# Down projection of a decoder block in split fp32: every fourth weight residual formed by an accumulating DMA

## The chip, the cores and the metric

One core of one Trainium2 chip. The metric is the device time of one execution in microseconds (us), the median over runs. The engines are TensorE (PE), VectorE (DVE), ScalarE (ACT), GpSimd (POOL) and SyncE (SP), each with its own queue of instructions; 16 DMA engines move data between HBM and the on-chip memory.

## The reference, cut to what matters

A decoder block on x of 256 x 2048, float32: a token-mixing part with three branches, then an MLP with a squared ReLU.

```python
h = rmsnorm(x, norm_ffn_g[l])
x = x + jnp.square(jax.nn.relu(h @ w_up[l])) @ w_down[l]
return rmsnorm(x, final_g)
```

`w_up` is 2048 x 8192 and `w_down` 8192 x 2048. The change touches only the product with `w_down`.

## The kernel before

**Split weights.** Each float32 operand is split into a rounded part (type float32r) and the residual. A product is the sum of three: rounded times rounded, rounded times residual, and residual times rounded. Weights come from HBM as slabs of 512 KB, and each goes through the same steps: SP loads it into `w_raw` (line 334 for `mix` and `down`, line 337 for the rest), ScalarE copies it rounded into `w_hi` (line 437, in `hi`), VectorE subtracts the rounded from the raw into `w_lo` (line 620, in `lo`), TensorE multiplies with `w_hi` and `w_lo`. All three are rings of 4 slots (`RING`); slab s lies in slot s % 4, and within every stage slot and index k in the trip agree.

**Order.** `walk` writes the order of stages for every engine: the mixing part (glu, short, kv, q, B, C, A, mix), then for each of four chunks of 2048 hidden columns an `up` stage of 4 trips with 8 slabs and a `down` stage of 2 trips with 16 slabs. Each engine goes through the same list, slab by slab. ScalarE and VectorE work 3 slabs ahead (`LOOKAHEAD`): at index k they make the rounded part and the residual of slab k + 3. In a `down` slab (line 1012, `products_as`) TensorE does 12 matmuls of 512 columns: 2 row blocks, 2 halves of the tokens, and 3 products each (lines 1026, 1027, 1028).

**Semaphores.** SP loads slab s after `lo_done` has reached s - 3, which says that the residual of slab s - 4, the previous one of its slot, is formed (line 332). ScalarE rounds slab s + 3 when its load has landed (`raw_full`) and TensorE is through with slab s - 1, the previous one of its slot (`slab_used`). VectorE waits for `hi_done`, TensorE for `lo_done` of its slab. SP's queue is in order: a load that waits holds back all loads behind it.

**Between up and down.** At the end of a group of an up stage ScalarE copies half of the sums (line 548), VectorE adds the other half, scales, squares (lines 901, 903, 949), ScalarE rounds the result into `m_hl` (line 589), and VectorE forms its residual (line 952). Only then do both go on to the next slabs. In a down stage VectorE adds the sums to `y_tok` once in 8 slabs (line 958).

**GpSimd** sums squares of x at the start of the kernel and has no instruction after that.

```python
dve.wait_ge(hi_done, s + (LOOKAHEAD + 1))
dve.tensor_tensor(w_lo[:, q], w_raw[:, q], w_hi[:, q].bitcast(F32), ALU.subtract).then_inc(lo_done, 1)
```

Of the kernel before, what the change touches and what calls it, by code (L numbers as in the profile page):

```python
# [21 lines left out]
F32 = mybir.dt.float32  # L22
F32R = mybir.dt.float32r
ACT = mybir.ActivationFunctionType
ALU = mybir.AluOpType
# [24 lines left out]
RING = 4  # L50
# [50 lines left out]
PH = plan()  # L101
CHUNKS = FF // D
# [51 lines left out]
    return ph.slab0 + k + t * ph.nslabs + c * CHUNK_SLABS  # L154


def group_of(ph, c, t, n):
    return ph.group0 + n + t * ph.ngroups + c * CHUNK_GROUPS

# [6 lines left out]
def build(nc, x, norm_mix_g, w_in, gate_b, conf_dw, conf_ln_g, conf_ln_b, w_conf_out, sconv_w,  # L166
# [5 lines left out]
    with ctx:  # L172
# [3 lines left out]
        def sem(name):  # L176
            return ctx.enter_context(nc.semaphore(name))


        w_raw = sb("w_raw", [P, RING, KT, COLS])  # L180
        w_hi = sb("w_hi", [P, RING, KT, COLS], F32R)
        w_lo = sb("w_lo", [P, RING, KT, COLS], F32R)
# [63 lines left out]


        raw_full = [sem(f"raw_full{i}") for i in range(RING)]
        hi_done, lo_done, slab_used = sem("hi_done"), sem("lo_done"), sem("slab_used")
        half_copied, half_sum, evac_done = sem("half_copied"), sem("half_sum"), sem("evac_done")  # L250

# [47 lines left out]
        def _(sp):  # L299
# [4 lines left out]
            def load_slab(ph, c, t, k):  # L304
                n, i, _ = ph.slabs[k]
                s = slab_of(ph, c, t, k)
                if ph.name in ("B", "C", "A"):
                    b = {"A": 0, "B": 1, "C": 2}[ph.name]
                    col = t * (2 * COLS) + (n // 2) * COLS
                    if n % 2:  # L310
                        w = (w_conf_out, w_sconv_out, w_attn_out)[b]
                    else:
                        w, col = w_in, col + (C_G + b * D)
                    row = i * ROWS
                else:
                    w, starts = {"glu": (w_in, (C_AVAL, C_AGATE)), "short": (w_in, (C_C, C_BH, C_B)),
                                 "kv": (w_in, (C_K, C_V)), "q": (w_in, (C_Q, C_Q + COLS)),
                                 "mix": (w_mix_out, (0, DCOLS)), "up": (w_up, (0, COLS)),
                                 "down": (w_down, (0, DCOLS))}[ph.name]
                    step = DCOLS * 2 if ph.name in ("mix", "down") else COLS * (1 if ph.name in ("glu", "short") else 2)  # L320
                    col = t * step + starts[n]
                    row = i * (DROWS if ph.name in ("mix", "down") else ROWS)
                    if ph.name == "up":
                        col = c * D + col
                    if ph.name == "down":
                        row = c * D + row

                shared = ph.name in ("B", "A")  # L330
                if not (isinstance(s, int) and s < RING or shared and k == 4):
                    sp.wait_ge(lo_done, s + (shared and k == 3) - (RING - 1))
                if ph.name in ("mix", "down"):
                    sp.dma_start(wide_rows(w_raw[:, k % RING]), w[bass.ds(row, DROWS), bass.ds(col, DCOLS)]
                                 .rearrange("(a p) n -> p a n", p=P)).then_inc(raw_full[k % RING], 16)
                else:
                    sp.dma_start(w_raw[:, k % RING], w[bass.ds(row, ROWS), bass.ds(col, COLS)]
                                 .rearrange("(a p) n -> p a n", p=P)).then_inc(raw_full[k % RING], 16)
# [47 lines left out]
        def _(pool):  # L386
# [33 lines left out]
            pool.wait_ge(fold1, 7)  # L420
            pool.tensor_tensor(merged[:, 0, :], merged[:, 0, :], merged[:, 1, :], ALU.add).then_inc(fold1, 1)


        @block.scalar
        def _(act):
            def hi(ph, c, t, k):

                s = slab_of(ph, c, t, k)
                if isinstance(s, int) and s + LOOKAHEAD >= TOTAL:
                    return  # L430
                ahead = k + LOOKAHEAD

                act.wait_ge(raw_full[ahead % RING], 16 * (ph.slab0 // RING + ahead // RING + 1)
                            + t * (16 * ph.nslabs // RING) + c * (16 * CHUNK_SLABS // RING))
                if not (isinstance(s, int) and s == 0):
                    act.wait_ge(slab_used, s)
                act.activation(w_hi[:, ahead % RING], w_raw[:, ahead % RING], ACT.Copy).then_inc(hi_done, 1)  # L437

            def start_pair(i):
                act.wait_ge(x_t, i + 1)  # L440
# [165 lines left out]
            for i in range(2):  # L606
                act.activation(yg_tok[:, 1, i * W2:(i + 1) * W2], yg_tok[:, 1, i * W2:(i + 1) * W2], ACT.Copy,
                               scale=tok_stat[:, 2, 1:2]).then_inc(scaled[1], 1)
# [3 lines left out]
        def _(dve):  # L612
            def lo(ph, c, t, k):
                s = slab_of(ph, c, t, k)
                if isinstance(s, int) and s + LOOKAHEAD >= TOTAL:
                    return
                q = (k + LOOKAHEAD) % RING

                dve.wait_ge(hi_done, s + (LOOKAHEAD + 1))
                dve.tensor_tensor(w_lo[:, q], w_raw[:, q], w_hi[:, q].bitcast(F32), ALU.subtract).then_inc(lo_done, 1)  # L620

            def prologue(s):
                dve.wait_ge(hi_done, s + 1)
# [359 lines left out]
        def _(pe):  # L983
# [28 lines left out]
            def products_as(ph, c, t, k):  # L1012
                n, i, size = ph.slabs[k]
                s, g, q = slab_of(ph, c, t, k), group_of(ph, c, t, n), k % RING

                pe.wait_ge(lo_done, s + 1)
                if i == 0:
                    pe.wait_ge(evac_done, g - 1)
                b = bank(ph, n)
# [188 lines left out]
```

## Time and profile before

| | us |
|---|---|
| median of 2 runs | 1557.16 (1557.07 to 1557.26) |
| the profiled execution, its own time | 1557.39 |
| its span in the trace | 1555.6 |
| TensorE busy | 1527.8 (98%) |
| VectorE busy | 1085.9 (70%) |
| ScalarE busy | 747.2 (48%) |
| GpSimd busy | 21.8 (1%) |
| DMA | 287.70 MB, mean 185 GB/s |

The profile is of one execution. Its span runs from the first to the last instruction on the engines, and the execution's own time is 1.8 us longer. A row of a group of instructions gives the line of the kernel, the engine, the operation, what is written from what, the shapes and the count, then busy time and mean duration; "idle before" is how long the engine stood still just before, with what ended the wait behind the arrow. PEld is TensorE's loading of weights, which overlaps its matmuls; SPq is SP's queue. PEclk is the granted clock of TensorE as a share of full speed.

### The profile page before, as it was taken

How to read it: one execution, taken by the hardware profiler on the slowest of the kernel's cores; microseconds unless marked ns; L12 is line 12 of the kernel's file. 1: busy time of each engine (PE TensorE's matmuls, PEld its weight loads, DVE VectorE, ACT ScalarE, POOL GpSimd, SP SyncE). 2: the span in 40 equal slices, each digit the busy share in tenths (PEclk: the TensorE clock that was granted, in tenths of full speed). 3: DMA queues.
4: the chain of work that ended last, by engine and by line, in shares of the span. 5: the costliest groups of instructions: out<-in, count | busy, mean ns of one | idle time of the engine just before them, and what ended most of it. 6: DMA issues, size and time to landing. Idle time of an engine off the chain costs nothing.

```text
span 1555.6 us, 23606 instructions
## 1 busy us (share of the span) xinstructions
PE 1527.8 (98%) x8231; PEld 1310.4 (84%) x8231; DVE 1085.9 (70%) x1407; ACT 747.2 (48%) x938; POOL 21.8 (1%) x27
## 2 busy tenths in 40 slices
PE   5999999999999999999999999999999999999997
PEld 4888888888888888888888888888888888888885
DVE  7658888999999988666556665466645665566653
ACT  4444444466664556545545444344433444344443
POOL 5000000000000000000000000000000000000000
PEclk9999999999999999999999999999999999999998
DMA  5666566745445665665556655565656565556553
GB/s 169 202 189 189 170 195 176 226 152 162 157 157 182 194 189 179 198 189 169 198 195 196 195 183 203 191 189 173 206 197 191 168 206 192 191 181 195 193 196 112
DMA packets 244855, 287.70 MB, mean 185 GB/s; under 512 B 9005, under 2 KB 202149, under 8 KB 244676
## 3 DMA queue, kind: packets, MB, share of 16 engines
q1 hardware_dynamic: 244804, 287.02, 57.9%
q8 instruction: 32, 0.52, 0.1%
q14 instruction: 19, 0.16, 0.0%
HBM read 284.36 MB, written 2.10 MB: 184 GB/s over the span
## 4 chain that ended last, share of the span: by engine, by line
PE 97%; DVE 2%; DMA 0%; ACT 0%; issue 0%; ACTq 0%; SPq 0%; DVEq 0%
PE acc L1009 42%; PE acc L1007 21%; PE acc L1028 9%; PE acc L1027 9%; PE acc L1026 9%; PE acc L1002 3%; PE acc L1004 2%; DVE h_hl L635 1%; PE acc L1032 1%; PE acc L1081 0%; DVE h_hl L631 0%; DVE w_lo L624 0%; DMA y_tok<-in_x 0%; PE acc L1104 0%; PE acc L1103 0%; PE acc L1102 0%
## 5 line engine op out<-in xcount | busy, mean ns | idle before, releaser
L620 DVE TENSOR_TENSOR w_lo<-w_raw,w_hi 128x1024 fp32r<-128x1024 f32 x533 | 643.4, 1222 | 283.6 <-ACT w_hi L437 280.2
L437 ACT ACTIVATE w_hi<-w_raw 128x1024 fp32r<-128x1024 f32 x533 | 555.5, 1055 | 462.3 <-PE acc L1009 243.7
L1009 PE MATMUL acc<-h_hl,w_hi 128*128 128x512 f32 x2460 | 775.1, 396 | 0.0
L1007 PEld LDWEIGHTS acc<-h_hl,w_lo 128*128 128x128 f32 x2460 | 456.8, 189 | 108.9 <-issue 6.3
L1007 PE MATMUL acc<-h_hl,w_lo 128*128 128x256 f32 x2460 | 487.6, 280 | 5.6 <-DVE w_lo L624 5.6
L1009 PEld LDWEIGHTS acc<-h_hl,w_hi 128*128 128x128 f32 x2460 | 376.3, 189 | 0.0
L1026 PE MATMUL acc<-w_hi,m_hl 128*128 128x512 f32 x640 | 249.2, 389 | 0.0
L1028 PE MATMUL acc<-w_hi,m_hl 128*128 128x512 f32 x640 | 249.0, 389 | 0.0
L1027 PE MATMUL acc<-w_lo,m_hl 128*128 128x512 f32 x640 | 249.0, 389 | 0.0
L1028 PEld LDWEIGHTS acc<-w_hi,m_hl 128*128 128x128 f32 x640 | 120.1, 188 | 24.9
L1027 PEld LDWEIGHTS acc<-w_lo,m_hl 128*128 128x128 f32 x640 | 120.2, 188 | 24.9
L1026 PEld LDWEIGHTS acc<-w_hi,m_hl 128*128 128x128 f32 x640 | 120.2, 188 | 24.9
L548 ACT ACTIVATE second<-acc 128x512 f32<-128x512 f32 x106 | 63.2, 596 | 159.7 <-PE acc L1009 159.7
L901 DVE TENSOR_TENSOR pair<-acc,second 128x512 f32<-128x512 f32 x94 | 64.9, 691 | 83.3 <-ACT second L548 83.2
L668 DVE SCALAR_TENSOR_TENSOR conv<-glu,par,conv (+1 forms) x240 | 109.1, 480 | 6.1 <-DVE conv L668 5.1
L1009 PE MATMUL acc<-z_ba,w_hi 128*128 128x512 f32 x224 | 70.4, 395 | 0.0
L903 DVE TENSOR_TENSOR pair<-pair,rstd 128x512 f32<-128x512 f32 x78 | 54.0, 692 | 2.7
L589 ACT ACTIVATE m_hl<-pair 128x512 f32 (+1 forms) x32 | 20.2, 632 | 74.1 <-DVE pair L949 74.1
L1002 PE MATMUL acc<-h_hl,w_hi 128*128 128x512 f32 x164 | 52.2, 399 | 3.4 <-DVE w_lo L624 3.4
L1007 PEld LDWEIGHTS acc<-z_ba,w_lo 128*128 128x128 f32 x224 | 40.7, 188 | 8.2
L952 DVE TENSOR_TENSOR m_hl<-pair,m_hl 128x512 f32 (+1 forms) x32 | 22.2, 693 | 32.4 <-ACT m_hl L589 32.4
L1007 PE MATMUL acc<-z_ba,w_lo 128*128 128x256 f32 x224 | 44.5, 280 | 0.0
(151 smaller groups left out, 734.5 us busy)
## 6 DMA issues: line engine op xcount, KB each, us to landing
w_raw<-in_w_in SPq DMA_DIRECT2D x200, 512.0 KB, 3.6
w_raw<-in_w_up SPq DMA_DIRECT2D x128, 512.0 KB, 3.9
w_raw<-in_w_down SPq DMA_DIRECT2D x128, 512.0 KB, 4.2
w_raw<-in_w_mix_out SPq DMA_DIRECT2D x32, 512.0 KB, 4.1
w_raw<-in_w_sconv_out SPq DMA_DIRECT2D x16, 512.0 KB, 3.4
w_raw<-in_w_attn_out SPq DMA_DIRECT2D x16, 512.0 KB, 3.4
w_raw<-in_w_conf_out SPq DMA_DIRECT2D x16, 512.0 KB, 3.9
y_tok<-in_x SPq DMA_DIRECT2D x4, 512.0 KB, 6.4
```

Of the source, the lines that this page charges most:

```text
L437: act.activation(w_hi[:, ahead % RING], w_raw[:, ahead % RING], ACT.Copy).then_inc(hi_done, 1)
L548: act.activation(second[:, :, :], acc[:, b:b + 2, SEQ:], ACT.Copy).then_inc(half_copied, 1)
L620: dve.tensor_tensor(w_lo[:, q], w_raw[:, q], w_hi[:, q].bitcast(F32), ALU.subtract).then_inc(lo_done, 1)
L668: dve.scalar_tensor_tensor(dst, src, w, dst, ALU.mult, ALU.add).then_inc(step, 1)
L901: dve.tensor_tensor(dst, halves[0], second[:, :, :], ALU.add).then_inc(half_sum, 1)
L903: dve.tensor_tensor(dst, dst, scale, ALU.mult).then_inc(evac_done, 1)
L1002: pe.matmul(*wide[m], start=True, stop=False)
L1007: pe.matmul(*narrow[m], start=False, stop=False)
L1009: last = pe.matmul(*wide[m], start=False, stop=final)
L1026: pe.matmul(acc[:, b + m, :], h_h, hi[:, a, :], start=first, stop=False)
L1027: pe.matmul(acc[:, b + m, :], h_h, lo[:, a, :], start=False, stop=False)
L1028: last = pe.matmul(acc[:, b + m, :], h_l, hi[:, a, :], start=False, stop=final)
```

## The change

In the down stages, a slab in the last slot of the ring (k % 4 = 3, 8 slabs of 32 in each chunk, 32 in all) gets its residual in another way. ScalarE, right after it has rounded the slab into `w_hi`, writes the rounded negative of the raw slab into `w_lo` with a second copy of scale -1. GpSimd waits for that and issues one DMA from `w_raw` to `w_lo` that adds what it reads to what is there, so that `w_lo` holds the raw minus the rounded weights. VectorE skips these slabs, and its increment of `lo_done` for the next slab is 2, so that the count stays right. TensorE waits for the DMA's semaphore `lo_added` before such a slab. SP waits for it before it loads the slot anew, in the down stages, and at index 3 of the trips of an up stage (chunks 1 to 3). Nothing else changes; the `added` function counts these slabs.

```diff
@@ -152,6 +152,11 @@
 def slab_of(ph, c, t, k):
 
     return ph.slab0 + k + t * ph.nslabs + c * CHUNK_SLABS
+
+
+def added(ph, c, t, k):
+
+    return (c * PH["down"].trips + t) * (PH["down"].nslabs // RING) + k // RING
 
 
 def group_of(ph, c, t, n):
@@ -246,6 +251,7 @@
 
 
         raw_full = [sem(f"raw_full{i}") for i in range(RING)]
+        neg_done, lo_added = sem("neg_done"), sem("lo_added")
         hi_done, lo_done, slab_used = sem("hi_done"), sem("lo_done"), sem("slab_used")
         half_copied, half_sum, evac_done = sem("half_copied"), sem("half_sum"), sem("evac_done")
 
@@ -330,6 +336,11 @@
                 shared = ph.name in ("B", "A")
                 if not (isinstance(s, int) and s < RING or shared and k == 4):
                     sp.wait_ge(lo_done, s + (shared and k == 3) - (RING - 1))
+                if ph.name == "down" and k % RING == RING - 1:
+                    if not (isinstance(c, int) and isinstance(t, int) and added(ph, c, t, k) == 0):
+                        sp.wait_ge(lo_added, 16 * added(ph, c, t, k))
+                if ph.name == "up" and k == RING - 1 and not (isinstance(c, int) and c == 0):
+                    sp.wait_ge(lo_added, 16 * added(ph, c, 0, 0))
                 if ph.name in ("mix", "down"):
                     sp.dma_start(wide_rows(w_raw[:, k % RING]), w[bass.ds(row, DROWS), bass.ds(col, DCOLS)]
                                  .rearrange("(a p) n -> p a n", p=P)).then_inc(raw_full[k % RING], 16)
@@ -420,6 +431,16 @@
             pool.wait_ge(fold1, 7)
             pool.tensor_tensor(merged[:, 0, :], merged[:, 0, :], merged[:, 1, :], ALU.add).then_inc(fold1, 1)
 
+            def add_low(ph, c, t, k):
+
+                pool.wait_ge(neg_done, added(ph, c, t, k) + 1)
+                pool.dma_start(w_lo[:, RING - 1].bitcast(F32), w_raw[:, RING - 1], accum_op=ALU.add).then_inc(lo_added, 16)
+
+            for c in range(CHUNKS):
+                for t in range(PH["down"].trips):
+                    for k in range(RING - 1, PH["down"].nslabs, RING):
+                        add_low(PH["down"], c, t, k)
+
 
         @block.scalar
         def _(act):
@@ -435,6 +456,8 @@
                 if not (isinstance(s, int) and s == 0):
                     act.wait_ge(slab_used, s)
                 act.activation(w_hi[:, ahead % RING], w_raw[:, ahead % RING], ACT.Copy).then_inc(hi_done, 1)
+                if ph.name == "down" and ahead % RING == RING - 1:
+                    act.activation(w_lo[:, RING - 1], w_raw[:, RING - 1], ACT.Copy, scale=-1.0).then_inc(neg_done, 1)
 
             def start_pair(i):
                 act.wait_ge(x_t, i + 1)
@@ -615,9 +638,12 @@
                 if isinstance(s, int) and s + LOOKAHEAD >= TOTAL:
                     return
                 q = (k + LOOKAHEAD) % RING
+                if ph.name == "down" and q == RING - 1:
+                    return
 
                 dve.wait_ge(hi_done, s + (LOOKAHEAD + 1))
-                dve.tensor_tensor(w_lo[:, q], w_raw[:, q], w_hi[:, q].bitcast(F32), ALU.subtract).then_inc(lo_done, 1)
+                dve.tensor_tensor(w_lo[:, q], w_raw[:, q], w_hi[:, q].bitcast(F32),
+                                  ALU.subtract).then_inc(lo_done, 2 if ph.name == "down" and q == 0 else 1)
 
             def prologue(s):
                 dve.wait_ge(hi_done, s + 1)
@@ -1013,7 +1039,10 @@
                 n, i, size = ph.slabs[k]
                 s, g, q = slab_of(ph, c, t, k), group_of(ph, c, t, n), k % RING
 
-                pe.wait_ge(lo_done, s + 1)
+                if ph.name == "down" and q == RING - 1:
+                    pe.wait_ge(lo_added, 16 * added(ph, c, t, k) + 16)
+                else:
+                    pe.wait_ge(lo_done, s + 1)
                 if i == 0:
                     pe.wait_ge(evac_done, g - 1)
                 b = bank(ph, n)
```

## Rows read from the trace of the kernel before

**Rows 1.** The page: busy time of each engine; GpSimd in 40 equal slices.

```profile
PE 1527.8 (98%) x8231; PEld 1310.4 (84%) x8231; DVE 1085.9 (70%) x1407; ACT 747.2 (48%) x938; POOL 21.8 (1%) x27
...
POOL 5000000000000000000000000000000000000000
```

**Rows 2.** The page: the chain that ended last, by engine and by line.

```profile
PE 97%; DVE 2%; DMA 0%; ACT 0%; issue 0%; ACTq 0%; SPq 0%; DVEq 0%
PE acc L1009 42%; PE acc L1007 21%; PE acc L1028 9%; PE acc L1027 9%; PE acc L1026 9%; PE acc L1002 3%; PE acc L1004 2%; DVE h_hl L635 1%; PE acc L1032 1%; PE acc L1081 0%; DVE h_hl L631 0%; DVE w_lo L624 0%; DMA y_tok<-in_x 0%; PE acc L110
```

**Rows 3.** Windows over the four down stages (start:end, us; busy us and count).

```profile
core 0: us, PE busy (x) PEld busy (x) DVE busy (x) ACT busy (x) POOL busy (x), PEclk, DMA share, GB/s
929.00:1016.00 87.00, 87.00 (x387) 72.17 (x386) 46.05 (x44) 35.25 (x34) 0.00 (x0) 1.00 0.59 195
1104.00:1191.00 87.00, 87.00 (x385) 72.03 (x384) 45.36 (x42) 34.86 (x34) 0.00 (x0) 1.00 0.61 198
1281.00:1368.00 87.00, 87.00 (x385) 72.07 (x384) 45.46 (x43) 34.92 (x35) 0.00 (x0) 1.00 0.60 197
1457.00:1545.00 88.00, 87.14 (x385) 71.81 (x383) 46.16 (x47) 35.41 (x43) 0.00 (x0) 1.00 0.48 160
```

**Rows 4.** Waits in the second down stage: total us, times, longest.

```profile
ACT w_hi L437 <- PE acc L1028: 48.1, 29, 1.7
DVE w_lo L620 <- ACT w_hi L437: 37.8, 26, 1.5
```

**Rows 5.** Order of time, steady part of that stage: start, us, engine [idle before].

```profile
1112.57 1.06 ACT L437 ACTIVATE w_hi<-w_raw 128x1024 fp32r<-128x1024 f32 x1 [1.66 <-PE acc L1028]
...
1118.01 1.06 ACT L437 ACTIVATE w_hi<-w_raw 128x1024 fp32r<-128x1024 f32 x1 [1.66 <-PE acc L1028]
1120.72 1.06 ACT L437 ACTIVATE w_hi<-w_raw 128x1024 fp32r<-128x1024 f32 x1 [1.66 <-PE acc L1028]
1123.44 1.06 ACT L437 ACTIVATE w_hi<-w_raw 128x1024 fp32r<-128x1024 f32 x1 [1.66 <-PE acc L1028]
1119.10 1.23 DVE L620 TENSOR_TENSOR w_lo<-w_raw,w_hi 128x1024 fp32r<-128x1024 f32 x1 [1.49 <-ACT w_hi L437]
```

**Rows 6.** SP's issues of the down loads: of 1112 to 1190, and one of them.

```profile
L334 SPq FUSED_REGOPS  x23: 47/47/121, 1112.6 to 1172.3; - x23
L334 SPq MOVE w_raw<-in_w_down x23: 29/29/29, 1112.6 to 1172.3; - x23
L334 SPq DMA_DIRECT2D w_raw<-in_w_down x23: 372/373/387, 1112.7 to 1172.4; - x23
DMA to landing us min/median/max: 3.5/3.6/5.6
...
L334 SPq DMA_DIRECT2D w_raw<-in_w_down x1: 373/373/373, 1120.5 to 1120.5; - x1
```

**Rows 7.** Order of time at the entrance of that stage: TensorE, ScalarE, VectorE.

```profile
1104.19 0.39 PE L1026 MATMUL acc<-w_hi,m_hl 128*128 128x512 f32 x1
...
1107.42 0.63 ACT L589 ACTIVATE m_hl<-pair 128x512 f32 x1 [2.31 <-DVE pair L949]
1107.95 2.96 ACT L437 ACTIVATE w_hi<-w_raw 128x1024 fp32r<-128x1024 f32 x3
...
1108.30 0.69 DVE L952 TENSOR_TENSOR m_hl<-pair,m_hl 128x512 f32 x1 [1.02 <-ACT m_hl L589]
1109.03 3.50 DVE L620 TENSOR_TENSOR w_lo<-w_raw,w_hi 128x1024 fp32r<-128x1024 f32 x3
```

**Rows 8.** DMA issues (KB, us to landing); window while k_dup is copied (DMA share, GB/s).

```profile
k_dup<-pair SPq DMA_DIRECT2D x4, 128.0 KB, 2.4
...
270.00:271.00 1.00, 1.00 (x7) 0.87 (x6) 1.00 (x2) 0.82 (x1) 0.00 (x0) 1.00 0.86 202
```

**Rows 9.** Windows: the last two columns are the DMA share and GB/s.

```profile
1108.00:1110.00 2.00, 2.00 (x10) 1.65 (x10) 1.66 (x2) 2.00 (x4) 0.00 (x0) 1.00 0.04 12
1110.00:1112.00 2.00, 2.00 (x11) 1.65 (x10) 2.00 (x3) 0.91 (x1) 0.00 (x0) 1.00 0.11 22
1112.00:1114.00 2.00, 2.00 (x11) 1.65 (x10) 0.87 (x2) 1.06 (x1) 0.00 (x0) 1.00 0.92 293
1114.00:1116.00 2.00, 2.00 (x11) 1.65 (x10) 0.88 (x1) 0.71 (x1) 0.00 (x0) 1.00 0.98 339
1130.00:1180.00 50.00, 50.00 (x222) 41.39 (x222) 25.50 (x23) 19.10 (x18) 0.00 (x0) 1.00 0.60 195
```

**Rows 10.** Windows of the start: the third column from the end is the granted clock.

```profile
10.00:15.00 5.00, 1.97 (x8) 1.57 (x8) 4.90 (x5) 4.05 (x9) 4.40 (x4) 1.00 1.11 343
20.00:25.00 5.00, 3.77 (x22) 2.63 (x21) 4.79 (x7) 2.15 (x5) 2.90 (x4) 1.00 0.16 37
25.00:30.00 5.00, 1.32 (x8) 0.79 (x6) 4.90 (x4) 2.79 (x3) 4.78 (x5) 0.85 0.23 79
30.00:40.00 10.00, 8.11 (x38) 7.15 (x39) 8.66 (x12) 1.66 (x2) 0.66 (x1) 0.74 0.48 141
```

## The prediction, made before the changed kernel was run

> **What bounds the kernel now.** I read the page's busy times first, then the chain that ended last, then the windows of the four down stages, then the waits and the order of time inside one of them. The busy line puts TensorE at 98% of the span, VectorE at 70% and ScalarE at 48% [rows 1]; the chain gives TensorE 97% and VectorE 2% [rows 2]. In each of the four down stages (87 us) TensorE is busy for the whole stretch but for 0.86 us at the end of the last one, while VectorE works 45 to 46 us and ScalarE 35 us [rows 3]. So the subtraction that the change takes from VectorE is in nobody's way: the waits of the stage say that VectorE waits for ScalarE's rounding and ScalarE waits for TensorE to free a slot [rows 4]. A slab's matmuls set the pace. The roundings start at 1118.01 and 1120.72, so a slab takes 2.72 us, and four slabs, from 1112.57 to 1123.44, take 10.87 us [rows 5].
>
> **What is taken away.** There are 32 such slabs (k = 3, 7, 11, 15 of 16, two trips, four chunks). Each takes one subtraction of 1.23 us from VectorE [rows 5], 32 x 1.23 = 39 us of its 1086 us. VectorE has some 41 us of idle time in each down stage and TensorE waits for it nowhere there, so I count 0 us gained.
>
> **What is added, in ScalarE.** One more pass over the same tile. I price it as the rounding beside it, 1.06 us [rows 5]. ScalarE is idle for 1.66 us before each rounding in the steady part [rows 5], and the pass follows the rounding, so it delays no other rounding there; what it delays is its own slab's residual. The other bookkeeping (a wait on SP, a wait on GpSimd, VectorE's increment of 2) carries no work. The increment of 2 makes the load of the next third-slot slab wait for the residual of the slab behind it, which is done at about 2.72 + 2.4 = 5.1 us after the third-slot rounding began; the added DMA ends later than that, so this wait is not the last. Below, T is the start of a third-slot slab's rounding, X the time from the end of the negated pass to the landing of the added DMA.
>
> **What is added, on the path of the residual.** Before, the residual of that slab is ready at T + 2.3 (1119.10 + 1.23 against 1118.01) and the next load of its slot is issued at T + 2.5 [rows 5, 6]. After, it is ready at T + 1.06 + 1.06 + 0.05 + X = T + 2.17 + X, the 0.05 us being one semaphore step. Two things wait for it.
>
> First, TensorE. In the steady part the rounding starts when slab s-1 of its slot is done, and TensorE comes to the slab three slabs later, at T + 8.1, so X may be 5.9 us. At the entrance of a down stage there is far less: the up stage's last evacuation holds ScalarE back, and the roundings of slabs 3, 4 and 5 come in a row from 1107.95; VectorE begins the residual of slab 3 at 1109.03 [rows 7]. Slab 0's matmuls begin at 1104.19 [rows 7], so slab 3 is due at 1104.19 + 3 x 2.72 = 1112.35. The negated pass would end at 1109.0 + 1.0 = 1110.0. **The first add has 2.3 us** before TensorE stands still, in each of the four chunks.
>
> Second, the slot. SP may not load the next slab into the third slot until the add has read the old one, and its queue is in order, so the loads behind it (slots 0, 1 and 2) are held too. The loop is: landing of a load 3.6 us (the median of 23 in this stage [rows 6]), rounding 1.06, negated pass 1.06, step 0.05, X, and 0.17 from release to issue: **X + 5.94 us** once round, against 10.87 us of matmuls. So X up to 4.9 us costs nothing in the steady part, and beyond it each of the seven later adds of a chunk costs X - 4.9 us. Held-back loads leave in a burst when the add lands.
>
> **How large is X.** The trace has no accumulating DMA and none issued by GpSimd. The nearest row is the copy inside on-chip memory, k_dup from pair: 128 KB land in 2.4 us [rows 8]. Beside it the engines moved 202 GB/s at a busy share of 0.86 [rows 8], so 131072 B are 0.65 us, and 1.75 us are fixed. The add has to fetch two operands of 524288 B each, 1.05 MB. At 339 GB/s, the best slice of the loads, that is 3.1 us; at 293 GB/s, the slice before it, 3.6 us; at the copy's 202 GB/s, 5.2 us [rows 8, 9]. From below, if the second operand cost nothing, 524288 B at 339 GB/s are 1.55 us. From above, 5.2 us at half the engines because loads run beside it, 10.4 us. X is thus between 1.75 + 1.55 = 3.3 and 1.75 + 10.4 = 12.1 us. I take the 293 GB/s of the loads, as the tile has rows of 4 KB, nearer to the loads' 2 KB packets than to k_dup's 1 KB rows: X = 1.75 + 3.6 = 5.3 us alone. At the entrance of a stage it is alone: the engines were busy for 0.04 and 0.11 of the slices from 1108 and 1110 [rows 9]. In the steady part it is not. The loads need 0.60 of the engines' time [rows 9], which is 6.5 us of each 10.87. Released together they start about 1 us after the release (0.17 us to the issue, and half of the 1.75 us fixed part) and run until 7.5 us after it; the next add's data starts 3.77 (release to landing) + 2.17 (rounding, pass, step) + 0.9 (half of the fixed part) = 6.8 us after it. The two share for the 0.7 us left and the add gets half, so I add 0.7, and 0.2 because SP needs 0.45 us for each load it issues (0.05 + 0.03 + 0.37 [rows 6]) and draws the burst out: X = 6.2 us.
>
> Where would the fixed part differ? The trace shows only DMAs of SP. The Trainium skill ("DMA: Bandwidth & Descriptors", Specifications) gives a first byte about 0.4 us later for DMAs issued by GpSimd than for those of SP; no row here shows it. By that alone the sum below would be 8 x 4 x 0.4 = 13 us more.
>
> **The sum.** Per chunk: first add 5.3 - 2.3 = 3.0 us; seven later ones (6.2 - 4.9) x 7 = 9.1 us, together 12.1. The steady part's own 5.9 us for TensorE is not an extra charge, since each lateness is carried on by the loop. After the last add of a chunk the up stage takes over; its third-slot load lands about 1 us late for its rounding and is due three slabs later, so it costs 0. Four chunks: 4 x 12.1 = 48 us. The profiled execution took 1557.39 us (span 1555.6), and the median shown is 1557.16, 0.2 us less, which I neglect: 1557.4 + 48 = **1605 us**.
>
> **Rivals.**
> - **The add fits the slack (not slower).** X up to 4.9 us, for instance 1.75 + 3.1 = 4.85. Then only the entrances cost: 4 x (4.85 - 2.3) = 10 us, 1568 us. With the lower bound of 3.3 it is 4 us, 1561 us. Up to X = 5.6 us the loss (8 x 5.6 - 2.3 - 34.3 = 8.2 us a chunk, near 31 us in all) stays about within 2%. For it: the engines have 0.4 of their time free, and every load already waits for a residual, so holding one back need not be felt. Against it: the loop has only 10.87 us, and load, rounding and pass use 5.94 of them before the add begins. The Trainium skill ("DMA: Bandwidth & Descriptors", Anatomy of one DMA) fits a GpSimd-issued copy by 2.0 us plus the bytes at 436 GB/s; an estimate from that page with both operands counted is 2.0 + 2.4 = 4.4 us, which is this case and would give 1566 us. No run here shows that fit.
> - **The add is much slower than two reads at the loads' rate.** If arithmetic in the DMA or the descriptors limit it, X = 9 us: 6.7 + 7 x 4.1 = 35 us a chunk, 142 us, 1699 us. At the upper bound of 12.1 us it is 4 x (9.8 + 50.4) = 241 us, 1798 us. For it: k_dup's copy ran at 202 GB/s, less than the loads, and nothing in the trace shows the DMA adding. Against it: the rows are long and all 16 engines have work.
> - **TensorE's stalls cost clock.** The granted clock is 1.00 in all down stages [rows 3]. It fell to 0.85 and 0.74 from 25 to 40 us, after TensorE had been busy 3.77 and 1.32 us of two stretches of 5 us [rows 10]; that is a mix of the 1.2 and the 2.4 GHz level. Stalls of 1 to 3 us in 12 leave TensorE much busier than that, and the clock stood at 1.00 from 10 to 15 us with 1.97 us busy [rows 10]. If the clock went to 0.74 for a tenth of the 348 us of the down stages, it would add 35 x 0.35 = 12 us to the forecast, 1617 us; for all of it 122 us.
> - **VectorE's relief pays (faster).** This needs TensorE to wait for VectorE in the down stages, or matmuls to run faster with fewer readers. The first is excluded by [rows 3, 4], the second has no row. If each of the 32 subtractions were on the path it would be 39 us, 1518 us.
> - **The change does not do what it says.** Only if GpSimd were held back by something else, which can't be: it does nothing after the first slice of the span [rows 1]. VectorE's count of residuals must fall by 32.
>
> **Chances.** Slower with X about 5.6 to 8 us, the forecast: 0.45. Add in the slack or barely beyond it: 0.35. Much slower add: 0.15. Clock on top of the forecast: 0.03. Faster: 0.02. A difference of 2% (31 us) is about what a measurement of this kernel can tell from no change; above it X must be over 5.6 us. So slower 0.63, within 2% 0.35, faster 0.02. The range goes from the lower bound's 1561 us to X = 9.3 us, 4 x (7.0 + 30.8) = 151 us, 1708 us.
>
> **What would show it.** TensorE's idle time in a down stage, now 0, should be some 12 us, named as waiting for the added DMA, 3 us of it before slab 3. The roundings of the third slot after the first should wait for their load, not for TensorE. GpSimd should show 32 DMAs of 512 KB with 5 to 7 us to landing. The up stages should stay as they are. VectorE should be 39 us less busy and ScalarE 34 us more. The forecast is wrong if the adds land in under 5 us, if they take over 8 us, or if TensorE's idle time lies where no add is waited for.

## The result and the profile after

The changed kernel takes 1590.22 us (median of 2 runs, 1590.04 to 1590.41) against 1557.16 us: the ratio is 1.021, 95% interval 1.0185 to 1.0234, or 33 us more. Four more runs beside seven of the kernel before gave 1591.34 us and a ratio of 1.022 (1.0202 to 1.0237). The forecast was 1605 us. The direction and the places of most of the loss came out as forecast, its size was 1.5 times too large.

The page of the changed kernel: busy times, the chain by engine and by line, and two groups.

```profile
span 1588.3 us, 23696 instructions
PE 1538.5 (97%) x8231; PEld 1310.2 (82%) x8231; DVE 1048.0 (66%) x1375; ACT 776.3 (49%) x970; POOL 49.4 (3%) x59
...
PE 80%; DMA 12%; ACT 3%; DVE 2%; issue 2%; ACTq 0%; SPq 0%; DVEq 0%
PE acc L1035 41%; PE acc L1033 20%; DMA w_lo<-w_raw 8%; DMA w_raw<-in_w_down 5%; PE acc L1055 4%; PE acc L1056 4%; PE acc L1057 4%; PE acc L1028 3%; ACT w_lo L460 2%; PE acc L1030 2%; DVE h_hl L661 1%; ACT w_hi L458 1%; PE acc L1061 1%; PE 
...
L645 DVE TENSOR_TENSOR w_lo<-w_raw,w_hi 128x1024 fp32r<-128x1024 f32 x501 | 604.6, 1222 | 339.9 <-ACT w_hi L458 336.7
L437 POOL DMA_DIRECT2D w_lo<-w_raw x32 | 27.6, 863 | 1510.8 <-ACT w_lo L460 1510.8
```

Against [rows 1], VectorE is 38 us less busy and ScalarE 29 us more. TensorE's share fell, but its busy time rose by 11 us. The table below finds 6.1 us of slabs that ran longer; the rest is about what 27 stalls add when a matmul's row of 0.39 us is no longer overlapped by the next after 0.23 us (an estimate). In [rows 2] the chain held no DMA worth 1%; now 12% of it is DMA, in two groups: the adds (w_lo from w_raw) and the loads for the down stages. The 32 adds take GpSimd 0.86 us each to issue.

The four down stages by windows, to compare with [rows 3].

```profile
core 0: us, PE busy (x) PEld busy (x) DVE busy (x) ACT busy (x) POOL busy (x), PEclk, DMA share, GB/s
934.00:1022.00 88.00, 84.25 (x361) 68.06 (x360) 33.59 (x31) 38.50 (x38) 6.65 (x8) 0.98 0.76 222
1110.00:1206.00 96.00, 90.95 (x396) 72.98 (x395) 37.05 (x37) 42.21 (x42) 6.87 (x8) 1.00 0.74 217
1294.00:1390.00 96.00, 90.89 (x394) 72.72 (x393) 36.79 (x37) 42.20 (x42) 6.88 (x8) 1.00 0.73 214
1478.00:1574.00 96.00, 88.64 (x377) 71.14 (x376) 35.63 (x37) 42.33 (x51) 6.88 (x8) 0.98 0.66 191
```

TensorE now stands still for 3.8 to 7.4 us of each window, the DMA share went from 0.60 to about 0.74 (in the last stage from 0.48 to 0.66), and in the first and last of them the granted clock is 0.98. These busy times hide a little, since a matmul's row is 0.39 us long and the next starts 0.23 us after it; I count stalls from the starts below.

The waits in the second down stage, to compare with [rows 4] (total us, times, longest).

```profile
ACT w_hi L458 <- DMA w_raw<-in_w_down: 27.9, 10, 5.3
ACT w_hi L458 <- PE acc L1057: 18.5, 14, 1.7
PEld acc L1055 <- DMA w_lo<-w_raw: 8.2, 8, 2.7
PE acc L1055 <- DMA w_lo<-w_raw: 5.0, 5, 2.3
```

Ten of the roundings wait for their load now, 27.9 us, where all had waited for TensorE, and TensorE waits for the add. The chain inside that stage, in order of time, with TensorE's own pieces between them left out (start, us, what; "issue" is time with nothing shown).

```profile
1115.43 1.05 ACT w_lo L460
1116.48 0.28 issue
1116.76 4.54 DMA w_lo<-w_raw
1121.52 3.81 DMA w_raw<-in_w_down
1125.47 0.12 ACT w_hi L458
1125.59 0.85 issue
1126.43 1.05 ACT w_lo L460
1127.48 0.28 issue
1127.77 4.89 DMA w_lo<-w_raw
1132.82 3.88 DMA w_raw<-in_w_down
1136.84 0.12 ACT w_hi L458
```

Here the loop of the forecast can be read off once round: an add issued at 1116.76 lands 4.54 us later, the held-back load takes 3.81 us, the rounding starts at 1125.47, the pass at 1126.43, and the next add is issued at 1127.77. The eight adds of this stage are issued from 1116.76 to 1196.62, seven rounds of 11.41 us on average, where four slabs of matmuls take 10.87.

TensorE at the entrance of that stage:

```profile
1118.66 0.39 PE L1057 MATMUL acc<-w_hi,m_hl 128*128 128x512 f32 x1
1121.35 0.50 PE L1055 MATMUL acc<-w_hi,m_hl 128*128 128x512 f32 x1 [2.30 <-DMA w_lo<-w_raw]
```

The last matmul of slab 2 starts at 1118.66 and would be followed at 1118.89; slab 3 starts at 1121.35, so 2.46 us are lost.

**Where the 33 us are.** From the starts of line 1055's matmuls I took, for each slab of the profiled execution, the time from its first matmul to that of the next slab, less 2.72 us, and kept what is over 0.1 us (stages numbered 1 to 4, slabs 0 to 31):

| us lost | stage 1 | stage 2 | stage 3 | stage 4 | sum |
|---|---|---|---|---|---|
| before slab 3 (entrance) | 2.70 | 2.47 | 2.47 | 2.55 | 10.2 |
| in slab 3 itself | 1.70 | 0.13 | 0.13 | 1.63 | 3.6 |
| before slabs 11, 19, 27 of the last stage | | | | 1.78, 1.77, 1.77 | 5.3 |
| before other third-slot slabs | 1.81 | 3.55 | 3.94 | 0.60 | 9.9 |
| first slab after a stall | 0.37 | 0.84 | 0.83 | 0.50 | 2.5 |

The stages take 93.1, 93.6, 93.9 and 97.2 us from the first to the last start of that line, against 86.4 before in each: 32.2 us of the 32.65 us between the two profiled executions (1590.04 and 1557.39). The table explains 31.5 of them. Its second, third and fifth rows were not in the forecast's sum.

**The three stalls of the last stage.** ScalarE there:

```profile
1501.71 1.06 ACT L458 ACTIVATE w_hi<-w_raw 128x1024 fp32r<-128x1024 f32 x1 [1.66 <-PE acc L1057]
1506.08 0.63 ACT L620 ACTIVATE square<-y_tok 128x512 f32<-128x512 f32 x1 [3.31 <-DVE y_tok L984]
1506.84 0.63 ACT L620 ACTIVATE square<-y_tok 128x512 f32<-128x512 f32 x1
1507.47 1.04 ACT L458 ACTIVATE w_hi<-w_raw 128x1024 fp32r<-128x1024 f32 x1
```

In the last chunk ScalarE also squares the finished outputs at the end of each group of 8 slabs (line 620). It waits for VectorE's sums for 3.31 us, squares until 1507.47, and only then rounds slab 11. That is the same lateness as at an entrance, and the add misses its due time by 1.8 us. The kernel before has the same order there, but its residual takes one subtraction of 1.23 us [rows 5] and came in time.

**The slow slabs.** Windows after the first stall of stage 1; the third column from the end is the granted clock.

```profile
936.00:940.00 4.00, 1.51 (x5) 1.31 (x6) 1.97 (x2) 1.06 (x1) 0.00 (x0) 0.91 0.51 107
940.00:944.00 4.00, 4.00 (x13) 3.10 (x13) 0.00 (x0) 0.84 (x1) 0.00 (x0) 0.67 0.96 304
940.00:942.00 2.00, 2.00 (x6) 1.51 (x6) 0.00 (x0) 0.00 (x0) 0.00 (x0) 0.50 0.96 292
944.00:948.00 4.00, 4.00 (x19) 3.27 (x19) 0.91 (x1) 2.23 (x3) 0.87 (x1) 1.00 0.85 262
```

TensorE had stood still for 2.7 us by its starts; then the clock fell to the 1.2 GHz level (0.50 from 940 to 942) and came back. Clocks of 0.91 and 0.67 over the two windows of 4 us make 0.7 and 2.6 us at that level, 3.4 us in all. This followed two of the four entrance stalls, and cost 1.5 to 1.6 us each (1.70 and 1.63 us in the table, less the 0.12 to 0.13 us of other restarts).

The adds in the list of DMAs (queue: packets, MB, share; then KB and us to landing), and the view of their own line.

```profile
q0 software_dynamic: 4608, 16.78, 5.5%
...
w_raw<-in_w_down SPq DMA_DIRECT2D x128, 512.0 KB, 5.2
w_lo<-w_raw POOLq DMA_DIRECT2D x32, 512.0 KB, 4.7
...
L437 POOL DMA_DIRECT2D w_lo<-w_raw x32: 850/859/1007, 933.7 to 1568.2; - x32
DMA to landing us min/median/max: 4.5/4.7/5.7
```

### The profile page after: what moved, and what is told of

Read it like the earlier page. It is cut to its first block, busy times and chain, and to the rows that moved or that the text cites. A ratio compares the mean times of both kernels' runs of the same rounds, so it can differ in the third digit from the quotient of the medians.

```text
span 1588.3 us, 23696 instructions
## 1 busy us (share of the span) xinstructions
PE 1538.5 (97%) x8231; PEld 1310.2 (82%) x8231; DVE 1048.0 (66%) x1375; ACT 776.3 (49%) x970; POOL 49.4 (3%) x59
## 4 chain that ended last, share of the span: by engine, by line
PE 80%; DMA 12%; ACT 3%; DVE 2%; issue 2%; ACTq 0%; SPq 0%; DVEq 0%
PE acc L1035 41%; PE acc L1033 20%; DMA w_lo<-w_raw 8%; DMA w_raw<-in_w_down 5%; PE acc L1055 4%; PE acc L1056 4%; PE acc L1057 4%; PE acc L1028 3%; ACT w_lo L460 2%; PE acc L1030 2%; DVE h_hl L661 1%; ACT w_hi L458 1%; PE acc L1061 1%; PE acc L1110 0%; DVE h_hl L657 0%
## 5 line engine op out<-in xcount | busy, mean ns | idle before, releaser
L645 DVE TENSOR_TENSOR w_lo<-w_raw,w_hi 128x1024 fp32r<-128x1024 f32 x501 | 604.6, 1222 | 339.9 <-ACT w_hi L458 336.7
L458 ACT ACTIVATE w_hi<-w_raw 128x1024 fp32r<-128x1024 f32 x533 | 555.4, 1055 | 465.8 <-PE acc L1035 238.4
L1055 PE MATMUL acc<-w_hi,m_hl 128*128 128x512 f32 x640 | 253.8, 396 | 21.3 <-DMA w_lo<-w_raw 21.1
L1057 PE MATMUL acc<-w_hi,m_hl 128*128 128x512 f32 x640 | 250.3, 391 | 0.0
L437 POOL DMA_DIRECT2D w_lo<-w_raw x32 | 27.6, 863 | 1510.8 <-ACT w_lo L460 1510.8
L984 DVE TENSOR_TENSOR y_tok<-acc,y_tok 128x512 f32<-128x512 f32 (+1 forms) x40 | 25.8, 687 | 30.2 <-PE acc L1057 30.2
```

Source lines behind the costliest of these rows:

```text
L1055: pe.matmul(acc[:, b + m, :], h_h, hi[:, a, :], start=first, stop=False)
L1057: last = pe.matmul(acc[:, b + m, :], h_l, hi[:, a, :], start=False, stop=final)
```

## The experiments

The changed kernel was run once more beside them.

> The changed kernel once more, for the spread of its time and for how often the slow clock follows a first stall: 1588 to 1592 us, with one to three of four entrances followed by a slab at the low level.

It took 1591.34 us, as given above; a slow slab followed three of its entrances.

The kernel before, measured beside each of the others, had medians of 1557.16 to 1557.76 us. Two theories were held against each other. Lateness: the loss is what the adds land after their due time, at an entrance, behind the squares, and through the loop. The rival: the adds' traffic, or the extra pass, costs by its amount.

**1. No add at all.** The residual of the 32 slabs is left as the negated rounded weights, TensorE waits for the pass, and SP's waits for the add are gone.

```diff
-                    pe.wait_ge(lo_added, 16 * added(ph, c, t, k) + 16)
+                    pe.wait_ge(neg_done, 16 * added(ph, c, t, k) + 16)
 ...
-                        add_low(PH["down"], c, t, k)
```

> Leaves out: the accumulating DMA; in those 32 slabs the residual is just the negated rounded weights. ScalarE's extra pass stays, TensorE waits for that pass instead of for the DMA, SP's wait for the DMA is gone, and VectorE still skips its 32 subtractions. If the whole loss comes from the time of the DMA (lateness theory), nothing is late: 1556 to 1560 us. If ScalarE's pass or the order of its queue costs something (rival), part of the 33 us stays: 32 passes of 1.04 us on the path would be up to 1590 us. If VectorE's relief of 39 us is worth anything, the time falls below 1555 us.

Measured: 1557.95 us, ratio 1.0002 (0.9993 to 1.0011). No slab of any down stage starts late. So the pass on ScalarE costs nothing, and 38 us less work on VectorE bring nothing: everything lost is in the DMA or in waiting for it.

**2. The first third-slot slab of each trip back to VectorE** (24 adds are left).

```diff
-                if ph.name == "down" and ahead % RING == RING - 1:
+                if ph.name == "down" and ahead % RING == RING - 1 and k > 0:
 ...
-                if ph.name == "down" and q == RING - 1:
+                if ph.name == "down" and q == RING - 1 and k > 0:
                     return
```

> The first third-slot slab of each trip (k = 3) goes back to VectorE, 24 adds are left. Lateness theory: the four stalls before slab 3 (10.2 us), the slow clock after two of them (3 us) and one of the three late adds of the last chunk (1.8 us) go, and as each later add then starts from the full 8.1 us of lead and the trips are cut into runs of three adds, nearly all of the steady stalls (10 us) go too: 1560 to 1564 us, with two stalls of about 1.8 us left in the last chunk. Rival, the loss goes by the number of adds and their traffic: 24 of 32 adds leave three quarters of 33 us, 1582 us.

Measured: 1566.88 us, ratio 1.0059 (1.0042 to 1.0076). The entrances are clean, no slab runs slow, 1.78 and 1.76 us remain before slabs 11 and 27 of the last stage, and 4.4 us of small stalls are left, more than expected: the time lies 3 us above the expected range. A quarter of the adds carried 23 of 33 us; the same cost for every add is excluded.

**3. The squares two slabs later.**

```diff
-                    if ph.name == "down" and isinstance(c, int) and c == CHUNKS - 1 and ends:
-                        j = 2 * t + n
+                    late = isinstance(c, int) and c == CHUNKS - 1 and ph.name == "down" and (
+                        k in (9, 15) if t == ph.trips - 1 and k >= 9 else k == 9 or k == 1 and t > 0)
+                    if late:
+                        j = 2 * t + (n if k == 15 else (0 if k == 9 else -1))
+                        g = group_of(ph, c, 0, j)
```

> Only ScalarE's order in the last chunk is changed: the sums of squares of an output group come two slabs later, so that they do not stand ahead of the rounding of a third-slot slab. Lateness theory: the three stalls of 1.8 us before slabs 11, 19 and 27 of the last chunk go, and a few steady ones of 0.5 us come in their place: 1585 to 1588 us. Rival, these stalls come from the adds' own length or from the load that arrives late: no change, 1590 us.

Measured: 1586.5 us, ratio 1.0192 (1.0175 to 1.0209), with runs from 1583.1 to 1589.3. The last stage fell from 97.2 to 91.1 us, and before slabs 11 and 27 no stall is left, before slab 19 one of 0.72. Of these 6.1 us, 1.5 are not the squares' doing: no slow slab followed the entrance of that stage in this execution. The median fell by 3.7 us.

**4. Both.** The edits of 2 and 3.

> The first third-slot slab of each trip (k = 3) goes back to VectorE, 24 adds are left, and in the last chunk the sums of squares come two slabs later. With k = 3 given back alone it took 1566.9 us, of which two stalls of 1.8 us stood before slabs 11 and 27 of the last chunk. Lateness theory: these go, some 0.3 us of steady stall may come for each: 1562.5 to 1564.5 us, the rest being steady stalls at the end of runs of three adds. Rival, ScalarE's order does not matter: 1566 to 1568 us.

Measured: 1561.83 us, ratio 1.0026 (1.0015 to 1.0036). The profiled execution is the slowest of eight, 1564.37 us. In its last stage no slab is late at all; the others lose 1.4 to 1.8 us each, mostly before slabs 15 and 31, where a run of three adds ends.

**5. The loop cut.** Slabs k = 7 and 15 go into another tile, so that their loads need not wait for the newest add.

```diff
+        def raw(ph, k):
+            if ph.name == "down" and k < ph.nslabs and k % (2 * RING) == 2 * RING - 1:
+                return w_sp[:, 0]
+            return w_raw[:, k % RING]
 ...
-                        sp.wait_ge(lo_added, 16 * added(ph, c, t, k))
+                    done = added(ph, c, t, max(k - RING, 0))
+                    if not (isinstance(done, int) and done == 0):
+                        sp.wait_ge(lo_added, 16 * done)
```

> Every second third-slot slab of a down stage (k = 7, 15) is loaded into a tile of its own (the place of the queries, which are done with), so SP waits not for the newest add but for the one before it, except once a trip (k = 3). All 32 adds stay. Lateness theory: the loop of load, rounding, pass and add is cut, nearly all steady stalls (10 us and the 0.13 us of each restart) go, and what stays is the entrance (10 us, and up to 3 us of slow clock) and the squares of the last chunk (5 us): 1574 to 1579 us. Rival, the adds' traffic slows loads and adds: the same bytes move beside the same loads, so the steady stalls stay, 1587 to 1592 us.

Measured: 1583.16 us, ratio 1.0168 (1.0152 to 1.0183), 4 us over the expectation. The steady stalls fell from 9.9 to 0.6 us, as the lateness theory has it. What was missed: the entrances grew to 3.15, 2.77, 2.79 and 2.88 us and the three later ones to 2.0 to 2.1 us, and three entrances were followed by a slow slab. The chain of this kernel at the second entrance, the pass and the add:

```profile
1113.63 1.05 ACT w_lo L467
1114.97 4.85 DMA w_lo<-w_raw
```

The add takes 4.85 us where it took 4.54. In this kernel the load of slab 7 is issued at 1117.19, before the add lands at 1119.82; in the changed kernel it is issued at 1121.52, after it. So traffic does cost, 0.3 us at this add, but by way of the add's due time.

**6. All three together** (2, 3 and the tile of 5, with SP's waits fitted to the 24 adds).

> All three together: slab k = 3 of each trip back to VectorE (24 adds left), the squares of the last chunk two slabs later, and k = 7 and 15 loaded into a tile of their own. Lateness theory: no add is due before it lands, so that the kernel is as the one before, 1557 to 1560 us, although 12.6 MB still go through the accumulating DMAs and ScalarE makes its extra passes. It cannot be faster than the kernel before, as TensorE waited for nobody in the down stages: a time under 1555 us would say that VectorE's relief (29 us here) is worth something. Rival, the traffic of the adds or the pass costs in itself: 24 of 32 of what is not explained by stalls, 1562 us or more.

Measured: 1558.39 us, ratio 1.0005 (0.9996 to 1.0014). Two down stages of this kernel by windows:

```profile
929.00:1016.00 87.00, 87.00 (x384) 71.81 (x383) 38.32 (x36) 40.61 (x40) 5.29 (x6) 1.00 0.75 223
1105.00:1192.00 87.00, 87.00 (x386) 72.01 (x385) 38.18 (x37) 40.55 (x40) 5.13 (x6) 1.00 0.76 225
```

TensorE works 87 of 87 us at a DMA share of 0.75 and a rate of 224 GB/s, with 24 adds in the way. The DMA share is that of the changed kernel (0.74), and without the lateness it costs nothing that can be measured. It is no faster than the kernel before either, though VectorE has 24 subtractions less.

**7. A copy in place of the add.** The residual is the raw slab, the addition is left out.

```diff
-                pool.dma_start(w_lo[:, RING - 1].bitcast(F32), w_raw[:, RING - 1], accum_op=ALU.add).then_inc(lo_added, 16)
+                pool.dma_start(w_lo[:, RING - 1].bitcast(F32), w_raw[:, RING - 1]).then_inc(lo_added, 16)
```

> Leaves out: the addition. The DMA from GpSimd copies the raw slab over the negated one, so the residual is the raw slab; everything waits as in the changed kernel. It tells what the second operand costs. My working (1.75 us fixed, the rest by bytes fetched, 1.05 MB): landing in 4.7 us falls to about 3.2 us, the loop of 11.2 us to 9.7 us, under 10.87 us, so that only the entrance (4 x 1.0 us) and little of the squares stay: 1560 to 1564 us. Rival, the issue and the descriptors of GpSimd make most of the time: landing 4.2 us or more, 1580 us or more.

Measured: 1564.23 us, ratio 1.0047 (1.003 to 1.0064), just above the expected range; stalls of 0.8 to 1.2 us at the entrances and none over 0.2 elsewhere. Its DMA queue, and the copies with their landing:

```profile
q0 software_dynamic: 4608, 16.78, 2.6%
...
L437 POOL DMA_DIRECT2D w_lo<-w_raw x32: 527/527/722, 933.3 to 1542.2; - x32
DMA to landing us min/median/max: 2.9/3.2/4.5
```

The median copy lands in 3.2 us as worked out, 1.5 us before the median add. Of these, 0.33 us are the shorter issue (527 against 859 ns). The queue's share gives the rest: 2.6% of 1561 us by 32 is 1.27 us of all 16 engines for a copy, 5.5% of 1588.3 by 32 is 2.73 us for an add.

Adding instead of copying is the price: it takes a second read and the arithmetic. No run here tells the two apart. The Trainium skill ("Collectives: The Full Stack", The bandwidth ceiling: the fold count and why AG ≠ RS ≠ AR) says of the reducing step of a collective that it is slower not for the add itself but for its two source reads, which halve the rate. The trace agrees in the factor, with 2.73 against 1.27 us.

**8. Half of each tile by the DMA, half by VectorE.**

```diff
-                pool.dma_start(w_lo[:, RING - 1].bitcast(F32), w_raw[:, RING - 1], accum_op=ALU.add).then_inc(lo_added, 16)
+                pool.dma_start(w_lo[:, RING - 1, 0:KT // 2].bitcast(F32), w_raw[:, RING - 1, 0:KT // 2], accum_op=ALU.add).then_inc(lo_added, 16)
 ...
```

> Half of each such tile (256 KB) goes through the pass and the accumulating DMA, VectorE subtracts the other half; TensorE waits for both. It gives a second point of the landing time against size. By bytes: landing falls from 4.7 to about 3.2 us, ScalarE's pass from 1.04 to 0.6 us, the loop from 11.2 to 9.3 us, and only the entrance stays at about 0.5 us each: 1559 to 1563 us. Rival, the fixed part is most of it: landing 4.1 us or more; then the entrance costs 1.4 us each, 1563 us or more.

Measured: 1563.71 us, ratio 1.0042 (1.0026 to 1.0059). The median landing of 3.7 us lies between the two theories. The issues of the adds of 256 KB and their landing:

```profile
L437 POOL DMA_DIRECT2D w_lo<-w_raw x32: 850/860/1010, 933.1 to 1540.4; - x32
DMA to landing us min/median/max: 3.3/3.7/5.9
```

The issue is as long as before. The fastest lands in 3.3 us, that of the full tile in 4.5. So 256 KB are worth 1.2 us, the full tile 2.4 us, and **2.1 us are fixed**; with two operands 1.05 MB in 2.4 us are some 430 GB/s. That is an estimate from two sizes, on times given to 0.1 us.

**9. The pass ahead of the rounding.**

```diff
-                act.activation(w_hi[:, ahead % RING], w_raw[:, ahead % RING], ACT.Copy).then_inc(hi_done, 1)
                 if ph.name == "down" and ahead % RING == RING - 1:
                     act.activation(w_lo[:, RING - 1], w_raw[:, RING - 1], ACT.Copy, scale=-1.0).then_inc(neg_done, 1)
+                act.activation(w_hi[:, ahead % RING], w_raw[:, ahead % RING], ACT.Copy).then_inc(hi_done, 1)
 ...
```

> ScalarE makes the negated pass before the rounding instead of after it; nothing else is changed (TensorE also waits for the rounding of such a slab, which ends long before the DMA). The add starts 1.0 us earlier. Lateness theory: the loop falls from 11.2 to 10.2 us, under the 10.87 us of four slabs, so the steady stalls (10 us) go; the four entrance stalls fall from 2.5 to 1.5 us and the three of the last chunk from 1.8 to 0.8 us, and no stall is long enough for the slow clock: 4 x 1.5 + 3 x 0.8 + 1 = 9.4 us over the kernel before, 1565 to 1569 us. Rival, the loss is the adds' traffic or their number: no change, 1588 to 1592 us.

Measured: 1582.63 us, ratio 1.0166 (1.0149 to 1.0183), far above the expected range. Half of it came true: the entrance stalls are 1.77, 1.52, 1.53 and 1.62 us, those of the last stage 0.83, 0.82 and 0.83, and no slab ran slow. The steady stalls did not go, they are 9 us. One round of the loop in the second stage:

```profile
1122.05 1.07 ACT w_lo L459
1123.11 0.28 issue
1123.40 5.80 DMA w_lo<-w_raw
1129.36 3.86 DMA w_raw<-in_w_down
1133.36 1.07 ACT w_lo L459
```

The add takes 5.80 us. The chain still needs 11.3 us a round. What the pass gave was taken by the landing, which rose from a median of 4.7 to 5.5 us. The likely reason: started 1 us earlier, the add meets more of the four loads that left together when the add before landed. In this round they were issued from 1118.18 to 1120.31 and landed until 1126.81, and the add ran from 1123.40.

**10 and 11. One load less in the burst.** SP issues the load of slot 0 ahead of that of the third slot, for k = 3, 7 and 11; 10 with the edit of 9, 11 without.

```diff
+                turn = list(range(ph.nslabs))
+                if ph.name == "down":
+                    for k in (3, 7, 11):
+                        turn[k], turn[k + 1] = k + 1, k
-                for k in range(ph.nslabs):
+                for k in turn:
```

> The pass ahead of the rounding, as in the swapped kernel (1582.6 us, where the adds took 5.5 us instead of 4.7 to land and the loop stayed at 11.3 us), and SP issues the load of slab k + 1 (slot 0) ahead of that of k for k = 3, 7, 11, so that one load less is held behind the add and released with it. Burst theory: the adds of the swapped kernel were late because they met the loads that the add before had held back; with a load less in the burst they land in about 4.8 us again, the loop is 10.2 us, under the 10.87 us of four slabs, and what stays is the entrances (1.5 us each), the squares (0.8 us each) and about 2 us: 1566 to 1571 us. Rival, the adds share the engines with whatever loads the pace of TensorE asks for, held back or not: adds still 5.5 us, 1580 to 1584 us.

> The changed kernel with only SP's order changed as above. Its adds already land in 4.7 us (median), so the burst theory expects little: the adds of 5.2 to 5.7 us become 4.7, the loop is 11.1 us, just over 10.87: steady stalls of 10 us become 4 to 7 us, 1584 to 1588 us. Rival as above: no change, 1590 us.

Measured: 1590.15 us, ratio 1.0199 (1.0181 to 1.0217), and 1597.69 us, ratio 1.0261 (1.0244 to 1.0278). Both are slower than without the edit, by 7.5 and 6 to 7.5 us, and outside both expected ranges. In 10, the add and the load that it releases, one after the other on the chain:

```profile
1131.61 4.58 DMA w_lo<-w_raw
1136.35 6.45 DMA w_raw<-in_w_down
```

Here the idea of the burst was half right: in 10 the add is down to 4.6 us, the median of all its adds too. But the load behind it takes 6.45 us instead of 3.9, and that gives back more. It is issued at 1136.35, 1.6 us after the load that was put ahead of it, which lands at 1138.34. The rival of the expectation did not come either, since it had the adds stay at 5.5 us. What fits all the kernels is that four loads and an add share the engines in each round, and that the one on the loop must not come second; in the order of the kernel as given, the load on the loop is the first of its burst. That reading is argued from these rows, and no run separates it further.

## Why the prediction was right, and where its sizes were off

- **No gain on VectorE, no cost of the pass.** Right: experiment 1, 1.0002. (ScalarE is 29 us busier and not 34: in the rows of the chain the pass starts 0.96 us after the rounding, while a rounding's row lasts 1.05.)
- **The entrances.** Right in place and nearly in size: 3.0 us each forecast, 2.55 measured on average. X alone is 0.28 us from the end of the pass to the issue and 4.54 us to the landing, 4.8 us, against 5.3. It is made otherwise than I worked it out: the fixed part is 2.1 + 0.28 = 2.4 us, not 1.75, and the data 2.4 us, not 3.6. I had taken the loads' 293 GB/s from HBM for reads inside the chip; [rows 8] and [rows 9] had nothing that runs at 430 GB/s. No run issues the same DMA from SP, so the 0.4 us of the prediction's sentence on GpSimd still has no row.
- **The loop.** This is the term that was mis-sized: 9.1 us a chunk, 36 us in all, against 9.9 us measured (and some of the 2.5 us of slower slabs after a stall). I took X = 6.2 us in the loop; the median is 0.28 + 4.7 = 5.0, the slowest 6.0. A round takes 11.41 us and not 12.14, and since only what lies over 10.87 counts, 0.7 us too much made it more than twice too large. The rest of the loop I had too short: 11.41 less 5.0 is 6.4 us, against 5.94. Most of that is the load, which lands in 3.6 to 4.7 us (median 3.9) in these 28 rounds, where I took 3.6.
- **Luck in the number.** X itself came out below what the forecast needed. It called itself wrong if the adds landed in under 5 us, and they landed in 4.7 us (median, from the issue). With the measured X its own sum gives 4 x (4.8 - 2.3) + 28 x (5.0 - 4.9) = 13 us, 1570 us, which is the rival of the hidden add. The measured 33 us came about because things that the sum had too small or not at all filled the place: the longer rest of the loop, the squares, the slow slabs and the restarts. TensorE's loss in a down stage was 6.7 to 10.8 us, where it had said some 12. The mechanism (first add late at the entrance, then a loop just over 10.87 us) is shown; that 1605 us lies near 1590 us is in part errors that cancel.
- **A second reason for the low price of the loop.** Where the entrance had cost a slow slab (stages 1 and 4), the stalls that followed are small (1.8 and 0.6 us), since the slow slab gives the loads time. In stage 4 the three stalls behind the squares do the same. The second profile, where the slow slabs fell in stages 2, 3 and 4, agrees: before other third-slot slabs its stage 1 lost 3.0 us without a slow slab (1.8 with one above), its stage 2 lost 2.3 with one (3.6 without). No run was made to separate it.
- **The squares of the last chunk.** Missed, and the step of the forecast that failed by its content and not by its size. I had counted one short lead per chunk, at the entrance, and taken all else for steady; the squares of the last chunk stand ahead of three roundings: 5.3 us. Experiments 3 and 4 show it.
- **The clock.** I had it as a rival of 0.03 with 12 us; some 3 us of the result are this, after two of four entrances. It is an addition, not another case.
- **The rival of the hidden add.** On X alone it was nearer than the forecast: X is over 4.9 us, but by 0.1 us. It had a chance of 0.35 and named 1566 us by the fit of the Trainium skill ("DMA: Bandwidth & Descriptors", Anatomy of one DMA). By that fit an add would land in 4.4 us (an estimate, with both operands counted); the fastest here took 4.5 and the median 4.7 from the issue. The time of 1566 us was too low because X begins 0.28 us earlier than the issue, and because of the squares, the clock and the loads' landing on the loop.
- **A cost by traffic.** Excluded as a cost in itself by experiment 6, and as the same cost for every add by experiment 2. It works through landing times (experiments 5, 9, 10 and 11).

The sum by its parts: 10.2 + 3.6 + 5.3 + 9.9 + 2.5 = 31.5 us of 32.65.

## What to carry to other kernels

Work moved onto a DMA from an engine that nobody waits for bought nothing here, and turned 1.2 us of latency into about 6 (a pass of 1.04 us and X of 5.0). Ask for two numbers before the throughput: how early the input is ready at every entrance (after an evacuation, behind any other work in the same queue, in the last chunk too), and how long the loop is from the slot's release back to its release; what exceeds the time of the ring's slabs is lost in every round. Where the loop is near its limit, shortening one part of it can be taken back by longer landings (experiment 9); a second buffer for the slot removed the loss in the loop (experiment 5), though not the one at the entrances.

## What the runs showed of the hardware that was not expected

- An accumulating DMA of 512 KB inside the chip, issued by GpSimd, lands in 4.5 us at best, a plain copy in 2.9 us; the issue takes 0.86 and 0.53 us. The adds' issue does not depend on the size (0.86 us for 256 KB).
- An entrance stall of TensorE of 2.5 to 3.2 us was sometimes followed by some 3.4 us at the 1.2 GHz level: after two, three, one, three and three of the four entrances in the changed kernel, its second profile, and the kernels of experiments 3, 5 and 11, 12 of 20 in all. None followed the stalls of up to 2.1 us. What decides among stalls of the same length stays open: the longest, 3.15 us in experiment 5, was not followed by it.
- After a stall the following slab mostly took 0.09 to 0.18 us longer (slabs after the small stalls in the two profiles of the changed kernel).
